# Turning a token block by scaled rows and a transpose instead of a diagonal product, at each norm of a two-layer decoder trunk

## The reference, cut to what matters

```python
def rmsnorm(x, g):
    y = x * lax.rsqrt(jnp.mean(x * x, axis=-1, keepdims=True) + EPS)
    return y * g

for layer in range(2):
    if layer % 2 == 0:   # mLSTM heads and causal pooling; first product h @ w_in
        x = x + even_mixer(rmsnorm(x, e_norm), ...)
    else:                # gated linear attention; first product h @ w_in
        x = x + odd_mixer(rmsnorm(x, o_norm), ...)
    # product keys: q = h @ w_q, top 16 of 128 x 128, softmax, then
    # a = h . u[experts], coef = g * gelu(a), y = coef . v[experts]
    x = x + peer_ffn(rmsnorm(x, f_norm[layer]), w_q[layer], keys[layer], u[layer], v[layer])
return rmsnorm(x, final_norm)
```

## Time and profile before

| | |
|---|---|
| median of 3 runs | 3931.47 us (3930.06 to 3933.08) |
| the profiled execution | 3927.91 us, its span 3926.1 us |
| TensorE busy | 3886.0 us, 99% of the span |
| VectorE busy | 2555.3 us, 65% |
| ScalarE busy | 2095.3 us, 53% |
| mean granted TensorE clock | 0.997 of full |
| data moved | 706.81 MB, 180 GB/s |

### The profile page before, as it was taken

The page is one execution under the profiler, slowest core; times in us unless marked ns, Lnnn a source line. Parts: engine busy times, 40 slices in busy tenths (PEclk is TensorE's granted clock), DMA queues, the critical chain, the costliest instruction groups (busy, mean ns, idle before and its releaser), DMA issues.

```text
span 3926.1 us, 72578 instructions
## 1 busy us (share of the span) xinstructions
PE 3886.0 (99%) x25540; PEld 3564.9 (91%) x25540; DVE 2555.3 (65%) x3844; ACT 2095.3 (53%) x3368; POOL 161.4 (4%) x140
## 2 busy tenths in 40 slices
PE   8999999999999999999999999999999999999999
PEld 7989999999998888888899879999999998888887
DVE  4565688788886555555554555787788885555555
ACT  5354444478885444444454444444588874444444
POOL 2110000010000000000121000000100000000000
PEclk9999999999999999999999999999999999999999
DMA  5445555555545565666444446555555555666665
GB/s 195 149 163 180 182 182 182 182 172 171 169 168 183 196 196 196 196 197 195 161 156 153 158 156 193 182 182 182 177 171 170 169 170 194 196 198 200 200 197 182
DMA packets 194871, 706.81 MB, mean 180 GB/s; under 512 B 22256, under 2 KB 22448, under 8 KB 194400
## 3 DMA queue, kind: packets, MB, share of 16 engines
q1 hardware_dynamic: 190800, 692.21, 53.6%
q0 software_dynamic: 3984, 13.37, 0.9%
HBM read 699.20 MB, written 6.29 MB: 180 GB/s over the span
## 4 chain that ended last, share of the span: by engine, by line
PE 95%; DVE 2%; DMA 2%; ACT 1%; issue 0%; SPq 0%; DVEq 0%; ACTq 0%
PE ps L1613 16%; PE ps L1614 16%; PE ps L1615 16%; PE ps L2001 12%; PE ps L2002 12%; PE ps L2003 12%; PE ps L1985 1%; PE ps L1696 1%; PE ps L1698 1%; PE ps L1697 1%; DMA w_raw<-in_dense 1%; DMA w_raw<-in_v_tab 1%; PE ps L1908 1%; PE ps L1910 1%; PE ps L1909 1%; DVE w_lo L1038 1%
## 5 line engine op out<-in xcount | busy, mean ns | idle before, releaser
L1038 DVE TENSOR_TENSOR w_lo<-w_raw,w_hi 128x1024 fp32r<-128x1024 f32 x1312 | 1628.9, 1243 | 1277.8 <-ACT w_hi L549 1262.4
L549 ACT ACTIVATE w_hi<-w_raw 128x1024 fp32r<-128x1024 f32 x1312 | 1389.1, 1060 | 1368.1 <-DMA w_raw<-in_v_tab 764.9
L1613 PE MATMUL ps<-act_lo_t,w_hi 128*128 128x256 f32 x5504 | 1562.5, 284 | 5.9 <-DVE act_lo_t L1097 3.6
L1614 PE MATMUL ps<-act_hi_t,w_lo 128*128 128x256 f32 x5504 | 1557.3, 283 | 0.0
L1615 PE MATMUL ps<-act_hi_t,w_hi 128*128 128x256 f32 x5504 | 1555.9, 283 | 0.0
L1613 PEld LDWEIGHTS ps<-act_lo_t,w_hi 128*128 128x128 f32 x5504 | 1053.2, 191 | 10.2 <-issue 7.1
L1615 PEld LDWEIGHTS ps<-act_hi_t,w_hi 128*128 128x128 f32 x5504 | 1054.7, 192 | 0.0
L1614 PEld LDWEIGHTS ps<-act_hi_t,w_lo 128*128 128x128 f32 x5504 | 1054.3, 192 | 0.1
L2001 PE MATMUL ps<-w_hi,act_lo_t 128*128 128x512 f32 x2048 | 798.5, 390 | 4.0 <-DVE act_lo_t L1519 3.0
L2002 PE MATMUL ps<-w_lo,act_hi_t 128*128 128x512 f32 x2048 | 797.0, 389 | 0.0
L2003 PE MATMUL ps<-w_hi,act_hi_t 128*128 128x512 f32 x2048 | 797.0, 389 | 0.0
(11 more groups left out here) (241 smaller groups left out, 2205.6 us busy)
## 6 DMA issues: line engine op xcount, KB each, us to landing
w_raw<-in_u SPq DMA_DIRECT2D x512, 512.0 KB, 3.3
w_raw<-in_v_tab SPq DMA_DIRECT2D x512, 512.0 KB, 3.9
w_raw<-in_dense SPq DMA_DIRECT2D x288, 512.0 KB, 3.3
x_spill<-big POOLq DMA_DIRECT2D x16, 256.0 KB, 4.4
big<-x_spill POOLq DMA_DIRECT2D x32, 128.0 KB, 4.3
big<-in_x_in SPq DMA_DIRECT2D x4, 512.0 KB, 5.3
big<-in_keys POOLq DMA_DIRECT2D x2, 1024.0 KB, 12.7
out<-big SPq DMA_DIRECT2D x8, 256.0 KB, 2.1
```

The source lines that it names most:

```text
L549: act.activation(w_hi[:, slot, :], w_raw[:, slot, :], ACT.Copy).then_inc(s_hi, 1)
L1038: dve.tensor_tensor(w_lo[:, slot, :], w_raw[:, slot, :], w_hi[:, slot, :].bitcast(F32), ALU.subtract).then_inc(s_lo, 1)
L1613: pe.matmul(out, wh, xl, start=start, stop=False, **kw)
L1614: pe.matmul(out, wl, xh, start=False, stop=False, **kw)
```

## The change

Three things change at each norm k = 0 to 3. The last norm only has other semaphore counts.

First, tb 1 gets no diagonal. VectorE multiplies its rows with the reciprocal in four instructions of 128 x 512 (into the second half of `HT`), and TensorE turns them with 16 transposes against the identity. Tb 0 keeps its diagonal and its 16 products. Second, the split of the first slab behind the norm is issued sooner: on ScalarE ahead of the last squares, on VectorE ahead of the additions that wait for the last products (for k = 1, 2 and 3; at k = 0 it stays). Third, VectorE's order in `norm` is now eight blocks of `turned_lo`, `lo` of slab n0 + 1, the other eight blocks, and `lo` of n0 + 2 and n0 + 3.

```diff
--- before.py
+++ after.py
@@ -338,6 +338,8 @@
         def xs(tb, c):
             return at(XT + D * tb + 512 * c, 512)
 
+        ROWS_AT, PER_NORM = HT + D, 5
+
         def rows_added(k, n):
 
             return 8 * (k - 1) + n
@@ -667,7 +669,6 @@
 
             def norm(k, n0):
 
-                hi(0, n0)
                 hi(1, n0 + 1)
                 turned_hi(k)
                 hi(2, n0 + 2)
@@ -683,6 +684,7 @@
                     if s % 8 == 3:
                         square(k, s // 8 * 2 - 2)
                         square(k, s // 8 * 2 - 1)
+                hi(0, SLAB0["wq", layer])
                 deviations(k, 6)
 
             def next_two(name, layer, b):
@@ -773,6 +775,7 @@
                 out_squares(0)
 
             def odd():
+                hi(0, SLAB0["qk", 1])
                 deviations(2, 4)
                 norm(2, SLAB0["qk", 1])
                 def gl_copy():
@@ -1016,7 +1019,7 @@
             odd()
             experts(1)
             deviations(4, 4)
-            act.wait_ge(s_diag, TB * 4 + 2)
+            act.wait_ge(s_diag, PER_NORM * 4 + 2)
             act.wait_ge(s_scaled, 2)
             for c in range(2):
                 act.activation(at(F_OUT + D + 512 * c, 512), at(F_SCALED + 512 * c, 512), ACT.Copy,
@@ -1068,6 +1071,7 @@
                             dve.tensor_tensor(xs(tb, g), xs(tb, g), bank(OUT_BANKS[layer][g % 2][tb]),
                                               ALU.add).then_inc(s_xadd, 1)
                 k = 2 * layer + 1
+                lo(0, SLAB0["wq", layer])
                 for tb in range(TB):
                     if tb == 0:
                         dve.wait_ge(s_ypart, 4 * layer + 1)
@@ -1084,6 +1088,11 @@
                 ins = dve.reciprocal(rroot[:, tb:tb + 1], root[:, tb:tb + 1])
                 if k == 4:
                     ins.then_inc(s_diag, 1)
+                elif tb:
+                    chain(ins)
+                    for c in range(4):
+                        dve.tensor_scalar(at(ROWS_AT + 512 * c, 512), xs(1, c), rroot[:, 1:2], None,
+                                          ALU.mult).then_inc(s_diag, 1)
                 else:
                     chain(ins)
                     dve.tensor_scalar(diag[:, tb, :], ident[:, :], rroot[:, tb:tb + 1], None, ALU.mult).then_inc(s_diag, 1)
@@ -1112,9 +1121,9 @@
 
             def norm(k, fill, n0):
 
-                lo(0, n0)
+                turned_lo(k, fill, range(8))
                 lo(1, n0 + 1)
-                turned_lo(k, fill)
+                turned_lo(k, fill, range(8, KB))
                 lo(2, n0 + 2)
                 lo(3, n0 + 3)
 
@@ -1576,6 +1585,8 @@
                     dve.wait_ge(s_last_gain, 16 * GAIN_PIECES)
                     dve.wait_ge(s_xadd, rows_added(k, 4))
                     scaled(0)
+                else:
+                    lo(0, SLAB0["qk", 1])
                 for n in range(4, 6):
                     add(n)
                 if layer == 1:
@@ -1587,7 +1598,7 @@
                                              scalar=rroot[:, tb:tb + 1], in1=at(F_GAIN + 512 * c, 512),
                                              op0=ALU.mult, op1=ALU.mult).then_inc(s_fin, 1)
                 if layer == 1:
-                    dve.wait_ge(s_diag, TB * k + 1)
+                    dve.wait_ge(s_diag, PER_NORM * k + 1)
                     finished(0, 0)
                     finished(0, 1)
                 add(6)
@@ -1597,7 +1608,7 @@
                     finished(0, 3)
                 deviation(k, 1)
                 if layer == 1:
-                    dve.wait_ge(s_diag, TB * k + 2)
+                    dve.wait_ge(s_diag, PER_NORM * k + 2)
                     finished(1, 2)
                     finished(1, 3)
 
@@ -1675,11 +1686,15 @@
 
             def turn(k):
 
-                for tb in range(TB):
-                    pe.wait_ge(s_diag, TB * k + tb + 1)
-                    for j in range(KB):
-                        pe.matmul(ps[:, j // 4 * 2 + tb, P * (j % 4):P * (j % 4 + 1)],
-                                  at(XT + D * tb + P * j, P), diag[:, tb, :], start=True, stop=True).then_inc(s_turned, 1)
+                pe.wait_ge(s_diag, PER_NORM * k + 1)
+                for j in range(KB):
+                    pe.matmul(ps[:, j // 4 * 2, P * (j % 4):P * (j % 4 + 1)], at(XT + P * j, P), diag[:, 0, :],
+                              start=True, stop=True).then_inc(s_turned, 1)
+                for j in range(KB):
+                    if j % 4 == 0:
+                        pe.wait_ge(s_diag, PER_NORM * k + 2 + j // 4)
+                    pe.transpose(ps[:, j // 4 * 2 + 1, P * (j % 4):P * (j % 4 + 1)], at(ROWS_AT + P * j, P),
+                                 ident[:, :]).then_inc(s_turned, 1)
 
             def out_gemm(layer, beside):
```

## The result

| | before | after |
|---|---|---|
| median of 8 runs each | 3930.59 us (3927.09 to 3933.42) | 3941.28 us (3937.78 to 3943.71) |
| ratio | | 1.0027 (95%: 1.0016 to 1.0038) |
| profiled execution (span) | 3927.91 (3926.1) | 3942.04 (3940.3) |
| mean granted clock | 0.997 | 0.994 |

The kernel became slower by 0.27%. A second comparison of the same two kernels gave 1.0019 (1.0010 to 1.0028); the mean of both differences is 9.4 us. I had forecast 3.8 us, in a range that ended at 3940.

What follows compares the result with a forecast made beforehand. TensorE was taken as the bound, with 95% of the chain of waits. Norms 0 to 3 summed to 0 + 0.74 + 2.3 + 0.74 = 3.8 us later, a median of 3935.3 us, range 3931 to 3940.

Steps and rivals of the forecast that it cites:

- The turn: tb 1 at each norm: 16 transposes take 1.8 us, 1.9 us less than the products; only the first four count.
- the four scalings: VectorE, tb 1's rows: about 0.5 us alone, 0.43 in a row, hidden at both rates considered, no cost.
- The 0.48 us: `turned_hi` and everything behind it can start 0.48 us sooner, as four transposes end after 0.44 us, not 0.92.
- The order: VectorE, `lo` between `turned_lo` halves: third slab 1.22 - 0.48 = 0.74 us later at norms 1 and 3, bounds 0.5 to 1.2.
- The sooner split: first slab's split ahead of the additions: hidden at norms 1 and 3 (0, bound 0.5), 1.4 us later at norm 2.
- Norm 2: split, turn and order together: 1.4 - 0.48 + 1.35 = 2.3 us later, between 1.9 and 3.6.
- Norm 0: VectorE's order stays and the quicker turn brings 0; bounds 0 and 1.2.
- The rival of the clock: clock falls behind the norms after transposes and idle time: up to 5.8 us on top, 3941 us; chance 20%.
- half clock behind a norm: sign against the forecast: granted clock at 0.5 behind a norm, where 1.0 was expected for 10 us.
- Nothing later gives time back: away from the norms: what follows is led by TensorE and its slabs, issued by its own progress; no term added.

Runs made afterwards that it cites:

- doubled: each of the 16 transposes issued twice: on the changed kernel 1.0012, +5.7 us; on the turn-only kernel 1.0003, +1.3 us.
- products at norm 0: the changed kernel with products with the identity at norm 0 alone, transposes at norms 1 to 3: 1.0012, +4.9 us against before.
- turn-only kernel: the kernel before with only tb 1's four scalings and 16 transposes: 1.0017, +6.9 us.
- order only: the kernel before with only VectorE's new order, the second slab's low part between the halves of `turned_lo`: 1.0003, +2.2 us.
- split only: the kernel before with only the sooner split of the first slab: 1.0005, +1.2 us.
- identity products: the changed kernel with its 16 transposes replaced by fp32 products with the identity: 1.0013, +4.6 us against before.

## Why the prediction was wrong

**The turn: right in size, and no gain alone.** 16 transposes take 1.78 us (forecast 1.8), the four scalings 1.68 (0.43 each was forecast in a row), and they are hidden. My rows fixed no rate for them (128 columns in 290 ns and 256 in 286), so that the 0.43 came so close has luck in it. The Trainium skill, "VectorE: DVE Perf Modes", in "The perf-mode tier table", gives an fp32 `tensor_scalar` from SBUF twice the rate of one from PSUM. The trace agrees: 0.42 us for 512 columns, where the row from PSUM has 0.48 for 256. The 0.48 us came as 0.46 where the split is sooner too, and as 0.01 where it isn't. **The order:** forecast +1.22 a norm, less 0.48; measured 1.13 alone, and 1.13 - 0.46 = 0.67 at norms 1 and 3 of all three builds that have the change's 16 transposes there and no spell (doubled, they give no head start, and it is 1.12). **The sooner split:** 0, 1.15, 0 alone, for 0, 1.4, 0. **Norm 2:** 1.25 to 1.85 in builds with the whole change, for 2.3, so below my lower bound of 1.9: the split alone gave 1.15 for 1.4, the order alone 0.96 for 1.35. **Norm 0:** 0 was forecast and can't be told: the first 100 us of single executions differ by -1.7 to +2.1 us from before's, and by 1.5 between two profiles of before. The three norms come to 2.6 to 2.75 us in the builds without a spell at norms 1 and 3, and those builds measured +2.8 and +2.9 (the one with products at norm 0: +4.9, 2.1 us more, which its interval allows). So at the norms my sum was some 1 us too high, a third of it.

**The rival of the clock: right in place, wrong in price.** I gave it 20% and up to 5.8 us. Its sign, half clock behind a norm, was one of those by which I said the forecast would be wrong, and its 3941 us is what was measured, but by luck: the spells account for some 0.6 to 1 us. It fell behind all four norms, for 3.4 us each rather than 6, and most of that lay in time that TensorE would have waited for VectorE's third slab anyway: 0.3 us a norm. In the old order, where that cover is missing, norms 1 and 3 of the turn-only kernel cost 1.4 us each. The Trainium skill, "TensorE: Matmul & The Clock Gate", Part 4, says transposes don't bring up the full clock. These runs don't bear it out for fp32 ones: 3.53 us of them and 1.03 to 1.20 us idle (4.6 to 4.7 us in all) left the clock up behind eight norms in two kernels, while 1.78 us of them and 2.34 to 2.95 us idle (4.1 to 4.7 us in all) were followed by a low spell behind 14 of 24 norms. That the idle time alone does it isn't shown: 2.35 and 2.46 us of it behind products, at norm 0 of the kernel before (second profile) and of order only, had no spell behind them, and no kernel has 1.78 us of transposes with a short idle stretch.

**The step that failed: "Nothing later gives time back", and with it a sum over norms alone.** I took it that away from the norms the kernel stays as it is, since its work does. It didn't: the dense slabs landed 0.4 to 0.5 us later, and three stretches with little in hand passed that on, 5.8 to 6.0 us. The profile before had the sensitive rows (where `hi` took the last held slab after 1.60 us of waiting for its DMA, became 2.68), but I asked of them only what the moved `hi` costs. My sum was 3.8; with this term it is 9.6, against 9.4 measured, of which 0.6 to 1 us is the clock's and as much was taken too high at the norms. No rival of mine had it.

**What is shown and what stays open.** Shown: the term goes when eight idle instructions are put behind all work or ahead of it, and comes to the kernel before when 32 products are taken out. The traces show this more sharply than the times: the 6.6 us are a difference between comparisons on several chips (+10.6 and +8.2 us against +2.9 and +2.8), and the kernels weren't run side by side. That the number of instructions is the cause, rather than something that goes with it (where the program or its data come to lie in memory, how its code is cut into pieces), isn't shown, and where between 72462 and 72494 the landing changes wasn't tried. Above 72494 the slab waits aren't always nothing either: 2.2 us in two profiles (split only, identity products), under 1.5 in the others; why is open. Why the `in_v_tab` slabs are spared is open too. All delays by stretch, the 0.3 us of a spell among them, are differences of single executions.

## What to carry to other kernels

Price an edit at its place, but then read the transfers of the whole kernel again: where a stage already waits for its slabs, as three do here, a landing time that moves by 0.4 us can cost more than the edit (here 5.8 us against 3.8). Before a loss (or a gain) of 0.2% is put down to what a change does, add a few idle instructions behind all work and see if it stays. Speeding up a producer gains only as far as the engine behind it is free then; look for what that engine has queued in the wait that you shorten.

## What the runs showed of the hardware that I had not expected

- A dense slab's median time to landing (512 KB) was 3.2 to 3.3 us in 16 profiles of 15 kernels and 3.7 to 3.8 in four profiles of three shorter ones (72450 and 72462 instructions); `in_u` slabs 3.2 to 3.3 against 3.6 to 3.7, the spill of 256 KB 4.3 to 4.4 us against 4.7 to 4.8. The `in_v_tab` slabs, also 512 KB, had 3.7 to 3.9 in all twenty.
- Eight one-column products at the end of TensorE's program made the changed kernel some 6.6 us faster (+2.8 in place of +9.4).
- A low spell of the clock behind a norm lasted 3.4 us each time. It followed 16 transposes and an idle stretch of 2.34 to 2.95 us behind 14 of 24 norms, and behind the other ten it didn't.
- An fp32 transpose of 128 x 128 costs one record of 0.11 us, an fp32 product of that size two.
- The four scalings ran in 1.68 us, and in 2.53 and 3.28 us at norm 0 in the two profiles of after, where GpSimd works beside them.
